# Host-packed per-feature vectors, one first stage with x loaded at its start, and projection weights in contiguous pieces

## The chip, the cores and the metric

The kernel runs on one core of one Trainium2 chip. A core has TensorE (PE), VectorE (DVE), ScalarE (ACT), GpSimd (POOL) and SyncE (SP), each with its own instruction stream, and 16 DMA engines. DMAs are issued here from SP's queue and from ScalarE's. The metric is the device time of one execution in microseconds (us), the median of the runs; less is better.

## The reference

A two-layer hybrid backbone serves 512 latent tokens and 128 context tokens of width 1024. Shortened to what matters here:

```python
def trunk_layer(x, mod, norms, mix_params, ffn, ctx):
    shift1, scale1, gate1, shift2, scale2, gate2 = jnp.split(mod, N_MOD, axis=-1)
    g_pre1, g_post1, g_pre2, g_post2 = norms
    h = rms_norm(x, g_pre1) * (1 + scale1) + shift1
    y, ctx_out = token_mixers(h, *mix_params, ctx=ctx)
    x = x + gate1 * rms_norm(y, g_post1)
    h = rms_norm(x, g_pre2) * (1 + scale2) + shift2
    return x + gate2 * rms_norm(ffn(h), g_post2), ctx_out

def token_mixers(h, w_in, conv_w, conv_b, ...):
    proj = h @ w_in                                    # (tokens, 1968)
    z, xbc, dt_raw, cq, ckv, k_rope = jnp.split(proj, ...)
    xbc = silu(centred_depthwise_conv(xbc, conv_w, conv_b))   # 5 taps
    ...                                                # chunked SSD scan
    q = rms_norm(cq, q_norm) @ w_uq
    ...                                                # latent attention
    return concatenate([rms_norm(y_ssd, ssd_norm), rms_norm(o, mla_norm)]) @ w_out
```

`mod` is SiLU(c) @ w_mod + b_mod, of 6 x 1024 values per layer, for `c` (latent tokens) and for `c_ctx` (context tokens). The feed-forward part is a dense SwiGLU in layer 0 and a top-2-of-8 expert SwiGLU in layer 1.

## The kernel before

All activations are float32. Tokens are tiled into five blocks of 128 (`TB` = 5; four latent, one context), features into eight of 128 (`KD` = 8). `build` (L2119) calls stages one after the other. Each stage is one block in which every engine has its own list of steps; semaphores (`Signal`) order steps of different engines, and a block ends when all of its engines have ended, so the stages are separated by barriers. Within a stage each engine takes its own list in order: a step that waits holds back all that is behind it in that list, DMA issues included.

The stages in order are: set-up, first modulation, and then for each layer pre-norm, input projection, SSD scan, attention, output projection, a second pre-norm, feed-forward and residual.

Set-up (`stage_setup`, L137) loads `c` and `c_ctx` feature-major into `silu_c` (values 4 bytes long, one per partition and column) on SP, builds identity and triangular masks on GpSimd, and takes SiLU on ScalarE.

First modulation (`stage_first_modulation`, L280) computes four units of 512 columns of `mod`: shift and scale of layer 0. The class `Modulation` holds this work in steps. `load` (on SP) brings each unit in four quarters of 128 x 1024 values (512 KB) into a ring of eight; a quarter past the eighth waits until TensorE has used the slots it replaces. `on_tensor` multiplies in two steps per unit (L230) and in a third transposes the unit's row (L218). `on_vector` copies the row out of PSUM (L240, `modrow`), and after the transposes sums it (L245) and adds the bias (L247), which needs `b_mod`. A unit's first product waits for the preceding unit's L247. `vectors` forms `scale_in` (L258). ScalarE issues ten loads of `b_mod` and gains in two layers, feature-major (L300, L302), then x_sample and x_prompt (L304, L305), then squares the five blocks of x (L428, through `squares_of`), and takes the root (L443). VectorE pads the SiLU values into `silu_wide`, makes float32r copies of two masks, waits for all ten small loads, runs the modulation steps and then `deviations` (L435 to L437), which turns sums of squares into `rstd`.

Pre-norm (`stage_pre_norm`) scales a diagonal by `rstd` (L397), multiplies each block of x by it (L382), evicts on VectorE (L411) and ScalarE (L364), and splits the result in a high and a low float32r part. SP loads the first two pieces of `w_in` (L473, class `InWeights`); in the input projection (`stage_in_proj`) it first issues five convolution tap rows and the bias (L511, L512), then pieces three to seven. A piece has 256 or 344 columns in eight row blocks; it is split on ScalarE (L478) and GpSimd (L482) and multiplied (L567, L570).

Attention (`stage_attention`) loads on SP `q_norm` (L1007), `kv_norm`, the rotary tables `cos` and `sin`, the cached latents and the weights, in this order; VectorE waits for the first four before it scales the latents (L1192). In layer 1 SP also writes zeros to the expert slots in DRAM. The output projection (`stage_out_proj`) loads `ssd_norm` and `mla_norm` (L1328, L1329), then four quarters of `w_out` (L1333), split in high and low parts on ScalarE and GpSimd (L1342); TensorE's products are L1404.

## Time and profile before

| | us |
|---|---|
| median of 3 runs | 2360.98 |
| lowest and highest | 2360.64, 2364.31 |
| the profiled execution, its time | 2356.16 |
| its span | 2354.4 |

| engine | busy us | share of the span |
|---|---|---|
| TensorE products | 2056.0 | 87% |
| VectorE | 1289.7 | 55% |
| ScalarE | 933.4 | 40% |
| GpSimd | 297.5 | 13% |

The page's list of DMA issues gives the time from issue to landing: 2.7 us for `c`, 8.0 us (median) for a quarter of `w_mod` in the first modulation, 8.2 us for x_sample and 8.9 us for x_prompt.

How to read the profile: times in rows are microseconds from the start of the span, unless marked ns. L240 is line 240 of the kernel before. A row of the timeline gives start, duration, engine, line, operation, written tile and read tiles, shapes, count, and in brackets the engine's idle time just before with what ended it. SPq and ACTq are the DMA queues of SyncE and ScalarE; the duration of a row with several issues runs from the first to the last. A row of stretches gives for each engine the busy time and the number of instructions, then the granted clock of TensorE as a share of 2.4 GHz, the busy share of the DMA engines (it can pass 1 in rounding), and the bytes moved. A busy time is no proof of a bound: what counts is which wait ends last in a stage.

### The profile page before, as it was taken

How to read it: one execution, taken by the hardware profiler on the slowest of the kernel's cores; microseconds unless marked ns; L12 is line 12 of the kernel's file. 1: busy time of each engine (PE TensorE's matmuls, PEld its weight loads, DVE VectorE, ACT ScalarE, POOL GpSimd, SP SyncE). 2: the span in 40 equal slices, each digit the busy share in tenths (PEclk: the TensorE clock that was granted, in tenths of full speed). 3: DMA queues.
4: the chain of work that ended last, by engine and by line, in shares of the span. 5: the costliest groups of instructions: out<-in, count | busy, mean ns of one | idle time of the engine just before them, and what ended most of it. 6: DMA issues, size and time to landing. Idle time of an engine off the chain costs nothing. (4 is left out here: it accounts for less than half of the span.)

```text
span 2354.4 us, 34297 instructions
## 1 busy us (share of the span) xinstructions
PE 2056.0 (87%) x12315; PEld 1777.1 (75%) x12315; DVE 1289.7 (55%) x1960; ACT 933.4 (40%) x1496; POOL 297.5 (13%) x128
## 2 busy tenths in 40 slices
PE   2898689985999999996998789797599999999992
PEld 1896447875999999996996448696487788778782
DVE  1735656654232022305817657643587888788884
ACT  1414203333221112104315103522577888788872
POOL 0220000031433233320320000300000000000001
PEclk9899899987999999997999899896799999999996
DMA  7315502110322122301306700201996835718444
GB/s 199 93 42 179 178 0 90 58 52 19 97 74 83 52 82 72 92 25 36 85 24 222 270 8 1 72 1 70 356 410 252 330 134 195 282 65 312 160 170 187
DMA packets 214206, 301.88 MB, mean 128 GB/s; under 512 B 52433, under 2 KB 143313, under 8 KB 214097
## 3 DMA queue, kind: packets, MB, share of 16 engines
q1 hardware_dynamic: 187744, 279.28, 33.8%
q10 hardware_dynamic: 23472, 10.57, 1.7%
q0 software_dynamic: 2880, 10.49, 1.1%
q8 instruction: 79, 1.29, 0.2%
q14 instruction: 31, 0.25, 0.0%
HBM read 358.20 MB, written 28.61 MB: 164 GB/s over the span
## 5 line engine op out<-in xcount | busy, mean ns | idle before, releaser
L1855 DVE TENSOR_TENSOR ex_wl<-ex_raw,ex_wh 128x1024 fp32r<-128x1024 f32 x364 | 425.3, 1219 | 57.7 <-ACT ex_wh L1734 53.7
L1734 ACT ACTIVATE ex_wh<-ex_raw 128x1024 fp32r<-128x1024 f32 x364 | 370.6, 1057 | 40.7 <-PE psum L1792 33.2
L1792 PE MATMUL psum<-ex_wh,ex_he_hi 128*128 128x512 f32 (+1 forms) x624 | 242.5, 389 | 5.1 <-DVE ex_wl L1855 5.1
L1792 PE MATMUL psum<-ex_wl,ex_he_hi 128*128 128x512 f32 (+1 forms) x624 | 233.3, 374 | 0.0
L1792 PE MATMUL psum<-ex_wh,ex_he_lo 128*128 128x512 f32 (+1 forms) x624 | 232.8, 373 | 0.0
L2001 POOL TENSOR_TENSOR ex_wl<-ex_raw,ex_wh 128x1024 fp32r<-128x1024 f32 (+1 forms) x60 | 160.6, 2679 | 338.4 <-ACT ex_wh L1987 338.4
L1044 ACT ACTIVATE at_prob<-psum,at_mx 128x640 f32<-128x640 f32 (+1 forms) x80 | 56.7, 708 | 307.2 <-DVE at_mx L1253 307.2
L2021 PE MATMUL psum<-h_hi,ex_wh 128*128 128x320 f32 x704 | 161.6, 311 | 16.7 <-POOL ex_wl L2001 15.3
L1987 ACT ACTIVATE ex_wh<-ex_raw 128x1024 fp32r<-128x1024 f32 (+1 forms) x60 | 68.4, 1141 | 259.9 <-PE psum L2021 243.0
L2021 PE MATMUL psum<-h_lo,ex_wh 128*128 128x320 f32 x704 | 161.3, 310 | 0.0
L2021 PE MATMUL psum<-h_hi,ex_wl 128*128 128x320 f32 x704 | 160.9, 310 | 0.0
L2049 DVE TENSOR_TENSOR ex_hf<-psum,ex_sg 128x640 f32<-128x640 f32 x22 | 18.1, 824 | 234.3 <-PE psum L2021 234.3
L1792 PEld LDWEIGHTS psum<-ex_wh,ex_he_hi 128*128 128x128 f32 x624 | 118.0, 189 | 27.7 <-issue 8.1
L1792 PEld LDWEIGHTS psum<-ex_wh,ex_he_lo 128*128 128x128 f32 x624 | 118.3, 190 | 21.9 <-issue 2.9
L1792 PEld LDWEIGHTS psum<-ex_wl,ex_he_hi 128*128 128x128 f32 x624 | 117.9, 189 | 21.0
L2021 PEld LDWEIGHTS psum<-h_hi,ex_wh 128*128 128x128 f32 x704 | 118.2, 189 | 17.2 <-issue 15.5
L2021 PEld LDWEIGHTS psum<-h_lo,ex_wh 128*128 128x128 f32 x704 | 118.5, 189 | 0.0
L2021 PEld LDWEIGHTS psum<-h_hi,ex_wl 128*128 128x128 f32 x704 | 118.5, 189 | 0.0
L1129 PE MATMUL psum<-mx_qkv_room,at_qT 96*128 96x320 f32 (+1 forms) x320 | 92.9, 416 | 13.8 <-DVE mx_qkv_room L1241 13.8
L1404 PE MATMUL psum<-op_w_hi,op_y_hi 128*128 128x256 f32 x320 | 93.2, 291 | 11.6 <-DVE op_y_lo L1431 11.4
L567 PE MATMUL psum<-win_hi,hm_hi 128*128 128x344 f32 (+1 forms) x320 | 96.4, 301 | 0.0
L567 PE MATMUL psum<-win_hi,hm_lo 128*128 128x344 f32 (+1 forms) x320 | 96.3, 301 | 0.0
(368 smaller groups left out, 4492.2 us busy)
## 6 DMA issues: line engine op xcount, KB each, us to landing
ex_raw<-moe_gate_up SPq DMA_DIRECT2D x286, 512.0 KB
ex_raw<-moe_w_down SPq DMA_DIRECT2D x78, 512.0 KB
x<-moe_w_down SPq DMA_DIRECT2D x65, 512.0 KB
wmod_ssd<-w_mod SPq DMA_DIRECT2D x56, 512.0 KB, 5.9
wmod_at<-w_mod SPq DMA_DIRECT2D x24, 512.0 KB, 4.9
ex_raw<-ffn_w_gate SPq DMA_DIRECT2D x22, 512.0 KB, 3.7
ex_raw<-ffn_w_up SPq DMA_DIRECT2D x22, 512.0 KB, 3.8
ex_raw<-ffn_w_down SPq DMA_DIRECT2D x16, 704.0 KB, 4.6
```

The costliest lines, as they stand in the source:

```text
L567: last = pe.matmul(p.psum[:, g % 8, 0:width], mh[:, k, j * P:(j + 1) * P], mw[:, k, :], start=first, stop=final)
L1044: act.activation(prob[:, n % 2, 0:hi - lo].rearrange("p (a k) -> p a k", a=2), p.psum[:, 2 * (n % 2):2 * (n % 2) + 2, 0:w], ACT.Exp, bias= ...
L1129: last = pe.matmul(p.psum[:, 2 * (n % 2) + part, 0:w], qT[0:QD, h, b * P:(b + 1) * P], kT[0:QD, h, lo + part * w:lo + (part + 1) * w], sta ...
L1404: last = pe.matmul(out, y[:, b % 2, k, :], w[:, i, k, :], start=(k == 0 and n == 0), stop=(k == KD - 1 and n == 2))
L1734: act.activation(wh[:, i % RING], raw_of(i), ACT.Copy).then_inc(*hi_done.up(1))
L1792: last = pe.matmul(p.psum[:, 2 + g % 2, 0:width], h[:, k], w[:, i % RING, cols], start=(k == 0 and m == 0), stop=(k == KD - 1 and m == 2))
L1855: dve.tensor_tensor(wl[:, i % RING], raw_of(i), wh[:, i % RING].bitcast(F32), ALU.subtract).then_inc(*lo_done.up(1))
L1987: act.activation(wh[:, SLOT[i], 0:size(i)], raw[:, i % 2, 0:size(i)], ACT.Copy).then_inc(hi_done, 1)
L2001: ins = pool.tensor_tensor(wl[:, SLOT[i], 0:size(i)], raw[:, i % 2, 0:size(i)], wh[:, SLOT[i], 0:size(i)].bitcast(F32), ALU.subtract)
L2021: last = pe.matmul(p.psum[:, 2 * PAIR[i] + half, 0:HT], w[:, SLOT[i], cols], m[:, k, half * HT:(half + 1) * HT], start=(k == 0 and n == 0) ...
L2049: ins = dve.tensor_tensor(hf[:].rearrange("p (a c) -> p a c", a=2), halves, sg[:].rearrange("p (a c) -> p a c", a=2), ALU.mult)
```

## The change

The host packs the following into one array `vectors` of 128 x 270 values: `c` and `c_ctx`, and for both layers `b_mod`, four gains, the convolution's taps and bias, `q_norm` and the norms of the two head groups. The kernel loads it once, on SP, and the tiles that held them become views of it. The set-up stage and the first modulation become one stage. In it SP issues the vectors and then `w_mod`; ScalarE issues x first, then takes SiLU, then squares x; VectorE does `deviations` before the modulation's steps instead of after them. The small loads of `stage_in_proj`, `stage_attention` (`q_norm`) and `stage_out_proj` go, with their waits. `w_mod`, `w_in` and `w_out` are laid out by the host so that each piece that is loaded is contiguous: 4 KB to 11 KB for each partition instead of runs of 1 to 2 KB. At the end of SP's list in attention a wait is added for the zeros that it wrote. No arithmetic of the reference moves to the host.

The diff, shortened; the GpSimd steps of set-up stand unchanged in the new stage.

```diff
+        self.vectors = sb("vectors_sb", [P, VECTOR_COLS])
+        self.silu_c = self.vectors[:, 0:2 * KD].rearrange("p (k s) -> p k s", k=KD)
...
@@ Modulation.load
             sp.dma_start(self.w[:, i % self.ring].rearrange("p (k f) -> p k f", k=QK),
-                         self.p.io["w_mod"][l, q * QK * P:(q + 1) * QK * P, u * UNIT:(u + 1) * UNIT].rearrange(
-                             "(k p) f -> p k f", p=P)).then_inc(*self.landed[i % self.ring].up(16))
+                         self.p.io["w_mod"][l, u, q].rearrange("p (k f) -> p k f", k=QK)
+                         ).then_inc(*self.landed[i % self.ring].up(16))
@@ stage_first_modulation
             @block.sync
             def _(sp):
+                sp.dma_start(p.vectors[:], io["vectors"]).then_inc(*vectors_in.up(16))
                 mod.load(sp)
...
             @block.scalar
             def _(act):
-                with nc.allow_non_contiguous_dma(reason="bias and gains, feature-major"):
-                    for l in range(2):
-                        act.dma_start(p.b_mod[:, l], io["b_mod"][l].rearrange("(k p) -> p k", p=P)).then_inc(*small.up(16))
-                        for j, name in enumerate(("norm_pre_mix", "norm_post_mix", "norm_pre_ffn", "norm_post_ffn")):
-                            act.dma_start(p.gains[:, l, j], io[name][l].rearrange("(k p) -> p k", p=P)
-                                          ).then_inc(*small.up(16))
                 act.dma_start(p.x[:, 0:LB], ...)
                 act.dma_start(p.x[:, LB], ...)
+                act.wait_ge(*vectors_in.at(16))
+                act.activation(p.silu_c, p.silu_c, ACT.Silu).then_inc(*silu_done.up())
                 for b in range(TB):
                     squares_of(p, act, b, junk[:], x_in.at(32), squared)
                 root_of_means(p, act, mean, root)
...
             @block.tensor
             def _(pe):
                 pe.wait_ge(*wide_ready.at(1))
+                pe.wait_ge(*consts.at(1))
...
             @block.vector
             def _(dve):
                 link = chained(dve_c)
-                pad_conditioning(p, link, dve, wide_ready)
+                link(dve, dve.memset(p.silu_wide[:], 0.0))
+                dve.wait_ge(*consts.at(1))
                 dve.tensor_copy(p.far_r[:], p.far[:])
                 dve.tensor_copy(p.ident_r[:], p.ident[:])
-                dve.wait_ge(*small.at(160))
+                dve.wait_ge(*silu_done.at(1))
+                dve.tensor_copy(p.silu_wide[:, :, 0:2], p.silu_c).then_inc(*wide_ready.up())
+                deviations(p, dve, squared, mean, root)
                 for step in range(len(mod.steps)):
                     mod.on_vector(dve, step)
                 mod.vectors(dve, link, 0, 0, ("scale",))
-                deviations(p, dve, squared, mean, root)
@@ InWeights.load
-        sp.dma_start(self.by_block(self.raw, i), self.p.io["w_in"][self.l, :, lo:hi].rearrange(
-            "(k p) f -> p k f", p=P)).then_inc(*self.landed[i % 2].up(16))
+        sp.dma_start(self.by_block(self.raw, i), self.p.io["w_in"][
+            self.l, :, KD * self.OFFSETS[i]:KD * self.OFFSETS[i + 1]].rearrange("p (k f) -> p k f", k=KD)).then_inc(...)
@@ stage_in_proj
-                    for k in range(TAPS):
-                        sp.dma_start(cw[:, :, k], io["conv_w"][l, k].rearrange("(f p) -> p f", p=P)).then_inc(*small.up(16))
-                    sp.dma_start(cb[:], io["conv_b"][l].rearrange("(f p) -> p f", p=P)).then_inc(*small.up(16))
                 for i in pieces[2:]:
                     w.load(sp, i)
...
-                act.wait_ge(*small.at(16 * (TAPS + 1)))
-                dve.wait_ge(*small.at(16 * (TAPS + 1)))
@@ stage_attention
-                    sp.dma_start(gq[:], io["q_norm"][l].rearrange("(k p) -> p k", p=P)).then_inc(*gains_in.up(16))
...
+                    sp.wait_ge(slots["cleared"], 16 * (MAX_BLOCKS + 1))
                 sp.wait_ge(*new_out.at(32))
...
-                dve.wait_ge(*gains_in.at(64))
+                dve.wait_ge(*gains_in.at(48))
@@ stage_out_proj
-                    sp.dma_start(gain[:, 0:4], io["ssd_norm"][l].rearrange("(k p) -> p k", p=P)).then_inc(*small.up(16))
-                    sp.dma_start(gain[:, 4:8], io["mla_norm"][l].rearrange("(k p) -> p k", p=P)).then_inc(*small.up(16))
-                    sp.dma_start(raw[:, i % 2], io["w_out"][l, :, i * quarter:(i + 1) * quarter].rearrange(
-                        "(k p) f -> p k f", p=P)).then_inc(*landed[i % 2].up(16))
+                    sp.dma_start(raw[:, i % 2], io["w_out"][l, i].rearrange(
+                        "p (k f) -> p k f", k=KD)).then_inc(*landed[i % 2].up(16))
...
-                dve.wait_ge(*small.at(32))
@@ build
-        stage_setup(p)
         stage_first_modulation(p)
@@ on the host
+def projection_pieces(a):
+    rows = a["w_in"].reshape(2, KD, P, IN_COLS).transpose(0, 2, 1, 3)
+    a["w_in"] = np.concatenate([rows[..., lo:hi].reshape(2, P, KD * (hi - lo)) for lo, hi in InWeights.PIECES], axis=2)
+    quarters = a["w_out"].reshape(2, KD, P, 4, D // 4).transpose(0, 3, 2, 1, 4)
+    a["w_out"] = np.ascontiguousarray(quarters.reshape(2, 4, P, KD * D // 4))
+    units = a["w_mod"].reshape(2, QUARTERS, QK, P, UNITS, UNIT).transpose(0, 4, 1, 3, 2, 5)
+    a["w_mod"] = np.ascontiguousarray(units.reshape(2, UNITS, QUARTERS, P, QK * UNIT))
```

## Rows read from the trace of the kernel before

**Rows 1.** Stretches: busy by engine PE, PEld, DVE, ACT, POOL; clock; DMA; GB/s

```profile
0.00:55.50 55.50, 14.65 (x80) 3.79 (x80) 5.50 (x19) 8.75 (x14) 2.31 (x13) 0.99 0.80 200
...
76.40:188.20 111.80, 111.10 (x768) 110.92 (x768) 52.93 (x63) 23.59 (x29) 32.40 (x9) 0.98 0.21 57
```

**Rows 2.** Waits before 56 us: who <- for whom: us, times, longest

```profile
ACT fm_junk L428 <- DMA x<-x_prompt: 40.5, 1, 40.5
DVE modrow_first L240 <- DMA gains<-norm_post_ffn: 31.6, 1, 31.6
```

**Rows 3.** Timeline, DMA issues: start, us, queue, line, destination<-source

```profile
0.79 0.45 SPq L146 DMA_DIRECT2D silu_c<-c  x1
...
4.55 39.65 SPq L209 DMA_DIRECT2D wmod_first<-w_mod  x16
...
5.05 20.41 ACTq L302 DMA_DIRECT2D gains<-norm_pre_mix  x1
...
35.06 0.61 ACTq L304 DMA_DIRECT2D x<-x_sample  x1
35.69 0.53 ACTq L305 DMA_DIRECT2D x<-x_prompt  x1
```

**Rows 4.** Timeline, first modulation: start, us, engine, work, [idle before <-releaser]

```profile
37.11 0.69 DVE L240 COPY modrow_first<-psum 128x512 f32<-128x512 f32 x1 [31.62 <-DMA gains<-norm_post_ffn]
...
39.45 3.64 PE L230 MATMUL psum<-wmod_first,silu_wide_first 128*32 128x512 f32 x16 [0.48 <-DVE mod L247]
...
44.61 1.06 ACT L428 ACTIVATE fm_junk<-x 128x1024 f32<-128x1024 f32 x1 [40.49 <-DMA x<-x_prompt]
...
45.05 1.92 PE L230 MATMUL psum<-wmod_first,silu_wide_first 128*32 128x512 f32 x16 [0.48 <-DVE mod L247]
...
48.92 2.20 PE L230 MATMUL psum<-wmod_first,silu_wide_first 128*32 128x512 f32 x16 [0.48 <-DVE mod L247]
...
50.31 0.18 ACT L428 ACTIVATION_READ_ACCUMULATOR fm_junk<-x 128x1 f32 x1
...
53.04 0.17 DVE L258 SCALAR_TENSOR_TENSOR scale_in<-mod,gains 128x16 f32<-128x16 f32 x1
53.25 0.17 DVE L435 TENSOR_SCALAR stat<-stat 128x5 f32<-128x5 f32 x1
...
55.52 0.48 DVE L397 TENSOR_SCALAR pn_diagonal<-ident,rstd 128x128 f32<-128x128 f32 x2 [0.30 <-PEq L290]
```

**Rows 5.** Stretches of 5 us: last column GB/s

```profile
5.00:10.00 5.00, 0.00 (x0) 0.00 (x0) 0.49 (x3) 0.00 (x0) 0.00 (x0) 1.00 0.93 225
...
20.00:25.00 5.00, 0.00 (x0) 0.00 (x0) 0.00 (x0) 0.00 (x0) 0.00 (x0) 1.00 1.11 342
...
40.00:45.00 5.00, 3.75 (x20) 0.81 (x12) 1.05 (x3) 0.39 (x1) 0.00 (x0) 1.00 1.03 412
```

**Rows 6.** Stretch in which the granted clock (PEclk) falls

```profile
54.00:55.00 1.00, 0.00 (x0) 0.00 (x0) 0.00 (x0) 0.99 (x2) 0.00 (x0) 0.53 0.00 0
```

**Rows 7.** Timeline, around and in the first pre-norm

```profile
51.92 0.66 PE L218 MATMUL psum<-ident,modrow_first 128*128 128x128 f32 x4 [0.80 <-DVE modrow_first L240]
...
59.69 0.46 ACT L364 ACTIVATE pn_h<-psum,mod,scale_in 128x128 f32<-128x128 f32 x1 [4.69 <-PE psum L382]
...
66.54 2.05 PE L382 MATMUL psum<-pn_diagonal,x 128*128 128x128 f32 x16 [0.75 <-DVE pn_diagonal L397]
```

**Rows 8.** Timeline, input projection: issue of the third piece

```profile
79.97 20.93 SPq L473 DMA_DIRECT2D mx_qkv_room<-w_in  x3
```

**Rows 9.** Waits of TensorE from 76 to 190 us

```profile
PE psum L570 <- PEq L340: 7.8, 1, 7.8
```

**Rows 10.** Timeline, first layer's attention

```profile
266.81 0.38 SPq L1007 DMA_DIRECT2D at_gq<-q_norm  x1
...
271.64 0.48 DVE L1192 SCALAR_TENSOR_TENSOR mx_ckr<-mx_ckr,at_rstd,at_kvrow 128x256 f32<-128x256 f32 x1 [3.07 <-DMA at_sin<-rope_sin]
```

**Rows 11.** Waits of TensorE in the second layer's output projection

```profile
PE psum L1404 <- POOL op_w_lo L1342: 0.3, 1, 0.3
```

More of the change, by code:

```diff
@@ L50 @@
 FAR = -1e30
+VECTORS = (("b_mod", NMOD * KD), ("gains", 4 * KD), ("conv_taps", XF * TAPS), ("conv_bias", XF), ("q_norm", QR // P),
+           ("group_norms", KD))
+LAYER_COLS = sum(n for _, n in VECTORS)
+VECTOR_COLS = 2 * KD + 2 * LAYER_COLS
 class Signal:
@@ L96, in __init__ @@
         self.far_r, self.ident_r = sb("far_r", [P, 2, P], F32R), sb("ident_r", [P, P], F32R)
-        self.silu_c = sb("silu_c", [P, KD, 2])
+        self.vectors = sb("vectors_sb", [P, VECTOR_COLS])
+        self.silu_c = self.vectors[:, 0:2 * KD].rearrange("p (k s) -> p k s", k=KD)
         self.mod = sb("mod", [P, 2, NMOD * KD, 2])
-        self.b_mod = sb("b_mod_t", [P, 2, NMOD * KD])
-        self.gains = sb("gains", [P, 2, 4, KD])
+        by_layer = self.vectors[:, 2 * KD:].rearrange("p (l c) -> p l c", l=2)
+        views, at = {}, 0
+        for name, n in VECTORS:
+            views[name] = by_layer[:, :, at:at + n]
+            at += n
+        self.b_mod = views["b_mod"]
+        self.gains = views["gains"].rearrange("p l (j k) -> p l j k", j=4)
+        self.conv_taps = views["conv_taps"].rearrange("p l (f t) -> p l f t", f=XF)
+        self.conv_bias, self.q_norm, self.group_norms = views["conv_bias"], views["q_norm"], views["group_norms"]
         self.scale_in = sb("scale_in", [P, 2, 2, KD, 2])
@@ L282, in stage_first_modulation @@
     nc, io = p.nc, p.io
-    x_in, small, dve_c = p.sig("x_in"), p.sig("mod_small"), p.sig("dve_chain")
-    wide_ready = p.sig("silu_wide_ready")
+    x_in, vectors_in, dve_c = p.sig("x_in"), p.sig("vectors_in"), p.sig("dve_chain")
+    consts, pool_chain, silu_done, wide_ready = (p.sig(n) for n in (
+        "consts", "pool_chain", "silu_done", "silu_wide_ready"))
     squared, mean, root = p.sig("x_squared"), p.sig("x_mean"), p.sig("x_root")
@@ L452 @@
     WIDEST = max(hi - lo for lo, hi in PIECES)
+    OFFSETS = [0, *itertools.accumulate(hi - lo for lo, hi in PIECES)]
     def __init__(self, p, l, raw_room, ctx):
@@ L501, in stage_in_proj @@
     with ExitStack() as own:
[L502 removed]
+        cw, cb = p.conv_taps[:, l], p.conv_bias[:, l]
         pad = p.sb(f"conv_pad{l}", [P, 2, PADW], ctx=own)
@@ L508, in _ @@
             def _(sp):
-                with nc.allow_non_contiguous_dma(reason="small per-channel vectors"):
-                    for k in range(TAPS):
-                        sp.dma_start(cw[:, :, k], io["conv_w"][l, k].rearrange("(f p) -> p f", p=P)).then_inc(*small.up(16))
-                    sp.dma_start(cb[:], io["conv_b"][l].rearrange("(f p) -> p f", p=P)).then_inc(*small.up(16))
                 for i in pieces[2:]:
@@ L1005, in _ @@
             def _(sp):
-                with nc.allow_non_contiguous_dma(reason="one gain per partition"):
-                    sp.dma_start(gq[:], io["q_norm"][l].rearrange("(k p) -> p k", p=P)).then_inc(*gains_in.up(16))
                 sp.dma_start(kvrow[:], io["kv_norm"][l].partition_broadcast(P)).then_inc(*gains_in.up(16))
@@ L1299, in stage_out_proj @@
     nc, io = p.nc, p.io
-    landed, small = [p.sig(f"weights_landed{i}") for i in range(2)], p.sig("wo_small")
+    landed = [p.sig(f"weights_landed{i}") for i in range(2)]
     hi_done, lo_done, y_out = p.sig("weights_hi"), p.sig("weights_lo"), p.sig("yt_out")
@@ L1326, in _ @@
             def _(sp):
-                with nc.allow_non_contiguous_dma(reason="one gain per partition"):
-                    sp.dma_start(gain[:, 0:4], io["ssd_norm"][l].rearrange("(k p) -> p k", p=P)).then_inc(*small.up(16))
-                    sp.dma_start(gain[:, 4:8], io["mla_norm"][l].rearrange("(k p) -> p k", p=P)).then_inc(*small.up(16))
                 for i in range(4):
@@ L2219 @@
     arrays["rope_cos"], arrays["rope_sin"] = rope_tables()
+    arrays["vectors"] = small_vectors(arrays)
+    projection_pieces(arrays)
     arrays["moe_gate_up"] = expert_pieces(arrays.pop("moe_w_gate")[0], arrays.pop("moe_w_up")[0])
```

72 lines of the change are left out of this document (36 added, 36 removed).

## The prediction

> **What bounds the kernel now.** I read four views, in this order. First the page's chain that ended last: nearly all of what it names is TensorE work of the expert stage, which the diff doesn't touch, so its shares don't answer the question. The stages stand one behind the other between barriers, so a stage that ends earlier moves all behind it by the same amount; each touched stage is therefore read alone, in the table of stretches. The first 55.5 us (set-up and first modulation) hold only 14.65 us of TensorE work, while the input projection is busy for 111.10 of 111.80 us [rows 1]. An earlier load can pay in the first and not in the second. Then the waits of the first stretch: ScalarE waits 40.5 us for `x_prompt`, VectorE 31.6 us for the last gain vector [rows 2]. The queue listing shows why. ScalarE's DMA queue starts with ten feature-major vectors (4-byte runs), and they block it: the issue of one gain takes 20.41 us, x_sample is issued at 35.06, x_prompt at 35.69 [rows 3]. Last the order of work in that stretch: two chains start late and end together. The modulation runs from the copy of unit 0's row at 37.11 to `scale_in`, 53.04 + 0.17 = 53.21. The norm runs from x landed (44.61) through five squares, to 50.31 + 0.18 = 50.49, and its next step stands on VectorE behind the modulation: 53.25 to 55.22, which is 0.30 before the next stage's first VectorE work at 55.52 [rows 4].
>
> **Part 1, vectors in one load, x first.** Removed: the ten vector loads ahead of x, and with them both waits of [rows 2]. Added: one load of 128 x 1,080 B ahead of w_mod on SP's queue. At the 2.7 us that c took it lands at 3.5, and even at twice that silu ends by 7 us, long before x. What is late next is x, since the change also puts `deviations` ahead of the modulation's VectorE steps: a new wait. Behind it on VectorE stand all twelve modulation steps, and TensorE waits for them from unit 0's transposes on. So the path is: x landed, norm, then the whole modulation.
> - x landed. Before, x took 44.61 - 35.06 = 9.55 us from its first issue [rows 3, 4]. 2.62 MB of x and an estimated 0.33 MB of w_mod went through in that time; at 0.41 MB/us, the mean of 40 to 45 us, once the 4-byte traffic is gone (342 GB/s with it beside [rows 5]), this is 7.2 us of transfer and 2.35 us fixed. After, both queues start at 0.79 [rows 3] and x meets eight w_mod quarters of 0.52 MB. Ends: x has the engines to itself, issued at 1.4 and landed 44.61 - 35.69 = 8.9 us later, at 10.3; or it is served behind all eight, 6.95 MB, 0.79 + 2.35 + 17.0 = 20.1. I take equal shares: 2 x 2.62 + 0.14 = 5.38 MB, 13.1 us, 0.79 + 2.35 + 13.1 = 16.2, less 0.2 for its head start: 16.0. The nearest row is x's own load, at whose end both queues had work too.
> - Norm: squares 50.49 - 44.61 = 5.9, mean to reciprocal 55.22 - 53.25 = 2.0 [rows 4]: VectorE free at 23.9.
> - Modulation: 53.21 - 37.11 = 16.1, less 0.3, the excess of unit 3's 2.20 over 1.92, which I read as its last quarters held up by x [rows 4]: 15.8, end 39.7. At 23.9 us at most twelve quarters and x, 9.05 MB, are asked for, 22 us of transfer; unit 2 needs the last of them some 8 us later. The modulation isn't bound by its loads.
> - Barrier 0.3: first VectorE work of the next stage at 40.0 instead of 55.52. Gain 15.5.
> Masks and silu now run inside this stage, under the load of x. Without that cover they would cost at most the 3.8 us between 0.79 and 4.55, the first issues of the two stages [rows 3].
>
> The Trainium skill (DMA: Bandwidth & Descriptors, "Where 436 GB/s comes from") puts loads from HBM at about 358 GB/s per core. By that x would land 1.9 us later (5.38/0.358 = 15.0 us against 13.1). The trace disagrees: 412 GB/s over five microseconds [rows 5]; the measurement decides. The same page ("Queues, rings and completion order") says that each DMA engine goes round its queues packet by packet, which would give the equal shares; no row isolates this for two queues of long runs.
>
> **Part 2, TensorE's clock at the next stage.** Before, TensorE's last transposes end at 51.92 + 0.66 = 52.58 and the granted clock falls early in 54 to 55 us (mean 0.53), to the 1.2 GHz level [rows 6]; the pre-norm starts cold and its first block is evicted at 59.69, 4.17 us after 55.52. Warm (2.4 GHz), a block's 16 records take 2.05 us [rows 7]; with 0.3 for the diagonal and 0.1 for the release that is 2.5. After, the norm's tail no longer stands between: the idle time is 0.63 (to `scale_in`'s end) + 0.3 + 0.3 = 1.2 us, under the 1.4 after which the clock fell, so I take it as warm: 1.7 us, and 0.3 of the second block's wait. Gain 2.0. Ends: 0 (it falls all the same) and 2.0. Inside the modulation unit 1 took 3.64 us and unit 2 1.92 [rows 4], which I read as cold and warm; a rise at another moment gains up to 1.7 or costs as much. I take none of that.
>
> **Part 3, input projections, both layers.** Six small loads go from ahead of the third piece, which is issued at 79.97 in a stage that starts at 76.4: 3.6 us of SP's queue [rows 8]. The cover is TensorE: its one wait from 76 to 190 us is the one for the stage's start [rows 9]. So nothing is gained; were the cover gone, it would be 3.6 us each. Contiguous pieces land earlier under the same cover, and so do the modulation weights of later stages. Gain 0; bounds -0.5 to +0.5 per layer.
>
> **Part 4, attention and output projection.** In attention VectorE's first scaling waits until 271.64 for the load of `sin`; ahead of it on SP's queue goes one issue of 0.38 us and its gap, 0.43 [rows 10], in two layers: 0.9. In the output projection of the second layer TensorE waits 0.3 us for a low part of w_out [rows 11]; w_out is now issued a microsecond earlier, its two gain loads gone: 0.3. The first product there waits for VectorE's `y_lo`, not for weights. The added wait for `cleared` ends SP's list in attention, with nothing of its stage behind it, and the stores it waits for are issued at the stage's beginning. Nothing.
>
> **Sum.** 15.5 + 2.0 + 0 + 0.9 + 0.3 = 18.7 us. The profiled execution has a span of 2354.4 and a time of 2356.16; after: 2335.7 and 2337.5. It ran 4.8 us under the median of the three runs, 2360.98; from that median: 2342.3.
>
> **Rivals.** (a) x nearly alone, landed at 10.3: 5.7 us more, 2336.6. For it: x is two issues, while w_mod's quarters go out one by one. Against: by 5 us both queues are full. (b) x behind w_mod, landed at 20.1: 4.1 us less, 2346.4; behind all twelve quarters at 25: 2351.3. For it: more is queued on SP. (c) As forecast, but the clock falls before the pre-norm: 2344.3; with (b) 2348.4. (d) Slower: the new wait itself. All of the modulation stands behind x; 7.9 + 15.8 + 0.3 us after x must still be before 55.52, so from x landed at 31.5 us on the first stage loses. That takes twelve quarters ahead of x and under 0.31 MB/us: at 225 GB/s, the mean of 5 to 10 us [rows 5], 9.05 MB land at 43.4, and the time is 2360.98 + 11.9 - 3.2 = 2369.7. Against: the 4-byte loads that stood beside that rate are gone. (e) The change doesn't do what its words say: contiguous w_mod, w_in and w_out bring nothing. That is already in the forecast; what carries it is ScalarE's queue [rows 3].
>
> **Chances.** Forecast 0.45, (c) 0.17, (a) 0.14, (b) 0.15, (d) 0.03, something that gives the gain back later 0.06. The range goes from (a) with an earlier rise of the clock, 2335, to (b) with (c) and some scatter of the median, 2350. A measurement of this kernel can tell about 0.2% (4.7 us) from no change: faster 0.93, same 0.04, slower 0.03.
>
> **What would show it.** The squares of x start near 16 us (10 to 20); the first `modrow` copy 7.9 us later; `pn_diagonal` near 40; a granted clock of 1.00 through the first pre-norm block, evicted 2.5 us after `pn_diagonal`; an input projection as long as before; attention's first scaling 0.43 us earlier in its stage. The prediction is wrong if the modulation waits for w_mod in units 1 to 3, if x is starved, or if a later stage grows.

## The result, and the profile after

The changed kernel takes 2345.32 us (median; 2338.96 to 2349.9), the kernel before 2360.81 in the runs beside it. The ratio is 0.9933, 95% interval 0.991 to 0.9955: 15.5 us faster. The forecast was 2342.3, with a range of 2335 to 2350. So sign, range and rough size hold. One step does not: two later stages give back 10 us by the traces, where the forecast had a gain of 0.3.

The profiled execution of the changed kernel was the slowest of its four (span 2348.1, time 2349.9), that of the kernel before (2356.16) quicker than all four of its other times. A second trace of the kernel before was taken for that reason (e10); its span is 2357.2. The table cuts both at the starts of the stages, read from the first DMA issue of each. In all listings below, rows between those shown are left out.

| stage | before, 2nd trace, us | after, us | difference | forecast |
|---|---|---|---|---|
| set-up and first modulation | 57.17 | 39.61 | -17.56 | -15.5 |
| pre-norm, input projection, layer 0 | 133.24 | 130.30 | -2.94 | -2.0 |
| SSD scan, layer 0 | 78.73 | 78.59 | -0.14 | 0 |
| attention, layer 0 | 197.75 | 196.31 | -1.44 | -0.43 |
| output projection, layer 0 | 115.19 | 119.63 | **+4.44** | 0 |
| up to layer 1's pre-norm | 522.78 | 522.90 | +0.12 | 0 |
| pre-norm to SSD scan, layer 1 | 212.14 | 212.44 | +0.30 | 0 |
| attention, layer 1 | 185.89 | 186.87 | +0.98 | -0.43 |
| output projection, layer 1 | 105.02 | 110.84 | **+5.82** | -0.3 |
| router, experts, end | 749.29 | 750.61 | +1.32 | 0 |
| whole span | 2357.2 | 2348.1 | -9.1 | -18.7 |

The first four rows bring 22.1 us, the two output projections cost 10.3. What is left, 2.7 us, is spread over four rows; 1.0 of it is attention in layer 1.

The stretches of the changed kernel that answer to [rows 1]; columns are length, then busy time and count of TensorE, its weight loads, VectorE, ScalarE, GpSimd, then granted clock, DMA share, GB/s:

```profile
0.00:39.60 39.60, 15.95 (x80) 4.35 (x80) 5.49 (x19) 8.73 (x14) 2.31 (x13) 1.00 0.71 282
58.20:169.90 111.70, 111.04 (x768) 110.84 (x768) 51.26 (x63) 23.70 (x29) 32.06 (x9) 0.98 0.17 57
```

The same engine work stands in 39.6 us instead of 55.5, and the input projection is as long and as full as it was. The waits before 40 us, answering to [rows 2] (who, for whom: us in total, times, longest):

```profile
ACT fm_junk L418 <- DMA x<-x_prompt: 10.3, 1, 10.3
...
DVE stat L425 <- ACT fm_junk L418: 16.0, 1, 16.0
```

ScalarE's wait of 40.5 us is 10.3 now. VectorE's wait for gains is gone, and the squares of x take its place. The timeline of that stage, answering to [rows 3, 4, 6, 7]:

```profile
13.98 1.06 ACT L418 ACTIVATE fm_junk<-x 128x1024 f32<-128x1024 f32 x1 [10.33 <-DMA x<-x_prompt]
...
19.88 0.17 DVE L425 TENSOR_SCALAR stat<-stat 128x5 f32<-128x5 f32 x1 [16.02 <-ACT fm_junk L418]
21.77 0.65 DVE L213 COPY modrow_first<-psum 128x512 f32<-128x512 f32 x1
24.08 3.64 PE L203 MATMUL psum<-wmod_first,silu_wide_first 128*32 128x512 f32 x16 [0.48 <-DVE mod L220]
30.14 2.97 PE L203 MATMUL psum<-wmod_first,silu_wide_first 128*32 128x512 f32 x16 [0.48 <-DVE mod L220]
35.07 1.93 PE L203 MATMUL psum<-wmod_first,silu_wide_first 128*32 128x512 f32 x16 [0.48 <-DVE mod L220]
38.93 0.17 DVE L231 SCALAR_TENSOR_TENSOR scale_in<-mod,vectors_sb 128x16 f32<-128x16 f32 x1
39.65 0.48 DVE L387 TENSOR_SCALAR pn_diagonal<-ident,rstd 128x128 f32<-128x128 f32 x2 [0.55 <-PEq L264]
42.08 1.50 ACT L354 ACTIVATE pn_h<-psum,mod,scale_in 128x128 f32<-128x128 f32 x4 [20.45 <-PE psum L372]
```

x lands at 13.98, the modulation starts 7.8 us later, its units 1 to 3 wait for VectorE and never for `w_mod`, and the first pre-norm block is evicted 2.43 us after `pn_diagonal`, at full clock:

```profile
35.00:40.00 5.00, 2.59 (x21) 0.85 (x21) 1.59 (x7) 0.00 (x0) 0.00 (x0) 1.00 0.00 0
40.00:42.00 2.00, 2.00 (x18) 2.00 (x19) 0.13 (x1) 0.00 (x0) 0.00 (x0) 1.00 0.69 168
```

Attention's first scaling, answering to [rows 10], starts at 252.44 in a stage that starts at 248.50: 3.94 us into it instead of 4.83; in layer 1, 3.89 instead of 4.29.

Now the stage that grows: layer 0's output projection in the changed kernel, by its timeline.

```profile
444.81 22.46 SPq L1313 DMA_DIRECT2D mx_qkv_room<-w_out  x4
449.60 1.89 POOL L1319 CAST op_w_hi<-mx_qkv_room 128x2048 fp32r<-128x2048 f32 x1 [200.53 <-DMA mx_qkv_room<-w_out]
451.57 4.50 POOL L1322 TENSOR_TENSOR op_w_lo<-mx_qkv_room,op_w_hi 128x2048 fp32r<-128x2048 f32 x1
452.75 3.34 DVE L1394 TENSOR_SCALAR op_stat<-op_stat 128x10 f32<-128x10 f32 x1
...
462.40 9.42 POOL L1322 TENSOR_TENSOR op_w_lo<-mx_qkv_room,op_w_hi 128x2048 fp32r<-128x2048 f32 x2 [6.33 <-ACT op_w_hi L1343]
...
467.50 5.40 DVE L1409 TENSOR_TENSOR op_y_lo<-op_yf,op_y_hi 128x1024 fp32r<-128x1024 f32 x1
...
472.95 0.58 PE L1384 MATMUL psum<-op_w_hi,op_y_hi 128*128 128x256 f32 x1 [10.15 <-DVE op_y_lo L1409]
```

Look at the ends, not the starts. A step on ten columns (`op_stat`, the mean of the squares) takes 3.34 us; it ends at 456.09, and GpSimd's first subtraction (`w_lo` of the first quarter of `w_out`) at 456.07. `y_lo` takes 5.40 us and ends at 472.90; the second and third subtraction run back to back (9.42 us) until 471.82, so it gets through 1.08 us after them. In the first trace of before the same two steps of this layer take 0.17 and 1.23 us. Between them stands the cast of `y_hi`, which is held as well (3.86 us; 0.69 where GpSimd is idle), but it was so in before too (3.77), so it is no part of the difference. The first product of the stage comes 28.1 us after its start (28.7 in layer 1), where it came after 21.8 and 21.1. TensorE's waits there:

```profile
PE psum L1384 <- DVE op_y_lo L1409: 10.2, 1, 10.2
...
PE psum L1369 <- ACT mx_xst L1338: 8.9, 1, 8.9
```

These two were 5.7 and 5.8 us in before: 4.5 and 3.1 us more, the two stalls one behind the other. All products of the stage then take 60.3 and 61.3 us instead of 62.6, so the stage as a whole loses 4.4 and 5.8 us and not 6.3 and 7.6. The granted clock helps in layer 0 alone, by some 0.8 us (it stays at the 1.2 GHz level for the first 3.1 us of the products instead of 4.7; in layer 1 for 5.2 instead of 3.6). What both layers share is a pace: at a granted clock of 1.00 a block of 96 products takes 11.46 us here and 11.76 in before. What that goes with is said under "What e3 adds".

### The profile page after: what moved, and what is told of

It reads as the page before. It is cut to its first block and busy times, and to the rows that moved or that the text cites. A ratio compares the mean times of both kernels' runs of the same rounds, so it can differ in the third digit from the quotient of the medians.

```text
span 2348.1 us, 34267 instructions
## 1 busy us (share of the span) xinstructions
PE 2051.2 (87%) x12315; PEld 1772.3 (75%) x12315; DVE 1305.1 (56%) x1960; ACT 934.9 (40%) x1496; POOL 294.3 (13%) x128
## 3 DMA queue, kind: packets, MB, share of 16 engines
q1 hardware_dynamic: 141488, 279.36, 32.7%
## 5 line engine op out<-in xcount | busy, mean ns | idle before, releaser
L2036 DVE TENSOR_TENSOR acc<-acc,psum 128x640 f32<-128x640 f32 x16 | 13.2, 822 | 149.6 <-PE psum L1999 149.6
```

## The experiments

Two theories stood at first. **P** (a conflict of VectorE and GpSimd): `w_out` lands earlier in its stage (its first quarter 4.79 us after the stage's start, before about 7.2), so GpSimd's subtractions come to lie on VectorE's two short steps, which then end only with them. **C:** the 10 us are scatter of the profiled executions, or a clock that fell. Later a third question came up: which part of the change carries the first stage's gain.

### e1: the changed kernel once more

> The changed kernel once more, beside which the others of this call are read. In its trace TensorE's first product of the output projection comes 28.2 us (layer 0) and 28.8 us (layer 1) after w_out's first issue, against 20.8 and 20.5 before; VectorE's op_stat took 3.34 and 4.26 us instead of 0.17 and 0.34, its op_y_lo 5.40 instead of 1.23. Theory P (a conflict of VectorE and GpSimd): the same again in every execution, since w_out's landing sets it, so the time is again about 15 us under before. Theory C (TensorE's clock and scatter between executions): the stage lengths differ from the first trace by several us in either direction.

Measured: 2345.98 us, ratio 0.9946 (0.9929 to 0.9962). `op_stat` 3.33 and 4.18 us, `y_lo` 5.40 twice, first product 28.15 and 28.77 us after the issue. The stalls are the same to 0.1 us in both layers: not scatter. C falls for them.

### e2: the output projection as it was before

```diff
+                    sp.dma_start(gain[:, 0:4], io["ssd_norm"][l]...)   # and mla_norm
-                    sp.dma_start(raw[:, i % 2], io["w_out"][l, i].rearrange(
-                        "p (k f) -> p k f", k=KD))...
+                    sp.dma_start(raw[:, i % 2], io["w_out"][l, :, i * quarter:(i + 1) * quarter].rearrange(
+                        "(k p) f -> p k f", p=P))...
...
+                dve.wait_ge(*small.at(32))
```

> The changed kernel with its output projection as before: w_out in rows of 1 KB and two gain loads issued ahead of it. Theory P: the first quarter lands 1.4 to 2 us later in its stage, GpSimd's first subtraction starts behind op_stat, the third one behind op_y_lo, both VectorE steps are short again (0.2 and 1.2 us), the first product comes 6 to 7 us earlier in each layer, and the time falls by 11 to 13 us against the changed kernel, about 27 us under before. Theory C: no change against the changed kernel beyond scatter (2 to 3 us).

Measured: 2337.08 us, ratio 0.9906 (0.9889 to 0.9923), 8.9 us less than e1, where 11 to 13 were expected. In the traces the two output projections are 11.4 us shorter than in e1; the first stage is 1.8 us shorter as well, which the edit doesn't touch (see Part 1). In its timeline the cast of the first quarter comes 7.25 us after the stage's start (443.76) instead of 4.79, and the stalls are gone:

```profile
451.01 1.89 POOL L1322 CAST op_w_hi<-mx_qkv_room 128x2048 fp32r<-128x2048 f32 x1 [203.00 <-DMA mx_qkv_room<-w_out]
451.75 1.18 DVE L1397 TENSOR_SCALAR op_stat<-op_stat 128x10 f32<-128x10 f32 x1
...
464.34 1.22 DVE L1414 TENSOR_TENSOR op_y_lo<-op_yf,op_y_hi 128x1024 fp32r<-128x1024 f32 x1
```

First product 20.87 and 20.42 us after the first issue for `w_out`. The give-back is made in this stage by this part of the change: the layout of `w_out` and the two gain loads with their tile `op_gain` of 128 x 8 values. e4 takes the first of these alone. (`op_stat` is 1.18 here because the cast lies on it until 452.90; that is short enough not to matter.)

### e3: the order held by two waits

The same kernel as the changed one, with contiguous `w_out` and its early landing kept; GpSimd may start the first subtraction only after `op_stat`, and the third only after `y_lo`.

```diff
                 for i in range(4):
                     pool.wait_ge(*hi_done.at(i + 1))
+                    if i == 0:
+                        pool.wait_ge(*mean.at(1))
+                    if i == 2:
+                        pool.wait_ge(*y_out.at(1))
```

> The changed kernel, in which GpSimd waits with its first subtraction for op_stat and with its third for the first op_y_lo; w_out lies as in the changed kernel. Theory P: as with the output projection of before, first product 6 to 7 us earlier per layer, 11 to 13 us off the changed kernel's time. A theory L (the contiguous layout itself makes w_out's later quarters slow) expects the third and fourth quarter to land late here too and no gain. Theory C: none either.

Measured: 2329.60 us (2328.03 to 2330.99), ratio 0.9876 (0.9859 to 0.9893), 16.4 us less than e1.

```profile
451.43 0.16 DVE L1398 TENSOR_SCALAR op_stat<-op_stat 128x10 f32<-128x10 f32 x1
451.74 4.51 POOL L1326 TENSOR_TENSOR op_w_lo<-mx_qkv_room,op_w_hi 128x2048 fp32r<-128x2048 f32 x1 [1.40 <-DVE op_stat L1398]
...
462.99 1.23 DVE L1413 TENSOR_TENSOR op_y_lo<-op_yf,op_y_hi 128x1024 fp32r<-128x1024 f32 x1
464.27 0.58 PE L1388 MATMUL psum<-op_w_hi,op_y_hi 128*128 128x256 f32 x1 [6.08 <-DVE op_y_lo L1413]
464.36 4.58 POOL L1326 TENSOR_TENSOR op_w_lo<-mx_qkv_room,op_w_hi 128x2048 fp32r<-128x2048 f32 x1 [1.96 <-DVE op_y_lo L1413]
```

Two waits that let the long instruction go second give back more than the whole of the loss: the stages take 111.1 and 101.2 us, against 119.6 and 110.8 in the changed kernel and 115.2 and 105.0 in before. Against before a stage is thus some 4 us shorter once nothing stands in the way of the early `w_out`: the first product comes up to a microsecond earlier, the products are 2 us shorter. Not all of that is the early `w_out` (see "What e3 adds"). P had expected 11 to 13 us, only the loss undone.

### e4: contiguous `w_out` alone, in the kernel before

```diff
-                    sp.dma_start(raw[:, i % 2], io["w_out"][l, :, i * quarter:(i + 1) * quarter].rearrange(
-                        "(k p) f -> p k f", p=P))...
+                    sp.dma_start(raw[:, i % 2], io["w_out"][l, i].rearrange(
+                        "p (k f) -> p k f", k=KD))...
```

> The kernel before with one part of the change: w_out in contiguous quarters, its two gain loads kept. Nothing is gained elsewhere. Theory P: the first quarter lands about 0.6 us earlier, so GpSimd's first subtraction starts at 8.6 instead of 9.2 us of its stage, at or before op_stat at 8.9 (it then takes 4 us); the third quarter is there 0.6 us earlier, so that the gap between the second and third subtraction, 1.0 us, shrinks to 0.4 and op_y_lo may miss it: 0 to 8 us per layer slower, in all 4 to 15 us slower than before. Theory C: same time as before.

Measured: 2367.86 us (8 runs), ratio 1.0043 (1.0029 to 1.0058): slower than before by 8.6 us, by nothing but a layout. The first quarter lands 0.6 us earlier in layer 0, and 0.4 to 1.1 us earlier in layer 1, by the trace of before that it is set against. The two layers separate the stalls. Layer 0, then layer 1:

```profile
473.35 4.49 POOL L1342 TENSOR_TENSOR op_w_lo<-mx_qkv_room,op_w_hi 128x2048 fp32r<-128x2048 f32 x1
473.69 4.18 DVE L1414 TENSOR_SCALAR op_stat<-op_stat 128x10 f32<-128x10 f32 x1
...
489.28 5.40 DVE L1431 TENSOR_TENSOR op_y_lo<-op_yf,op_y_hi 128x1024 fp32r<-128x1024 f32 x1
...
1515.63 4.55 POOL L1342 TENSOR_TENSOR op_w_lo<-mx_qkv_room,op_w_hi 128x2048 fp32r<-128x2048 f32 x1
1515.64 0.17 DVE L1414 TENSOR_SCALAR op_stat<-op_stat 128x10 f32<-128x10 f32 x1
...
1526.92 4.61 POOL L1342 TENSOR_TENSOR op_w_lo<-mx_qkv_room,op_w_hi 128x2048 fp32r<-128x2048 f32 x1 [0.30 <-ACT op_w_hi L1363]
1527.21 5.41 DVE L1431 TENSOR_TENSOR op_y_lo<-op_yf,op_y_hi 128x1024 fp32r<-128x1024 f32 x1
```

In layer 0 both stall and the first product comes after 28.99 us. In layer 1 `op_stat` starts within 0.01 us of the subtraction and gets through in 0.17; only `y_lo` stalls, and the first product comes after 24.14. Against 20.8 and 20.1 in before that is 8.2 us for two stalls and 4.0 for one. The same two pairs in the kernel before, layer 0:

```profile
473.41 0.17 DVE L1414 TENSOR_SCALAR op_stat<-op_stat 128x10 f32<-128x10 f32 x1
473.64 4.51 POOL L1342 TENSOR_TENSOR op_w_lo<-mx_qkv_room,op_w_hi 128x2048 fp32r<-128x2048 f32 x1
...
484.98 1.23 DVE L1431 TENSOR_TENSOR op_y_lo<-op_yf,op_y_hi 128x1024 fp32r<-128x1024 f32 x1
485.36 5.28 POOL L1342 TENSOR_TENSOR op_w_lo<-mx_qkv_room,op_w_hi 128x2048 fp32r<-128x2048 f32 x1 [0.96 <-ACT op_w_hi L1363]
```

`op_stat` started 0.23 us ahead of the subtraction (0.39 in layer 1), `y_lo` 0.38 us ahead of the third one: by so little the kernel before missed the two stalls.

### e5: x first, alone, in the kernel before

```diff
+                act.dma_start(p.x[:, 0:LB], io["x_sample"]...).then_inc(*x_in.up(16))
+                act.dma_start(p.x[:, LB], io["x_prompt"]...).then_inc(*x_in.up(16))
                 (the ten vector loads, and after them no x)
```

> The kernel before with one part of the change: ScalarE issues its two loads of x ahead of the ten feature-major vector loads; nothing else moves. Theory Q (the queue of 4-byte loads is the bound, through both x and the gains): x lands near 11 to 16 us, but VectorE's first modrow copy still waits for the last gain, issued 1.1 us later than before, and lands at 37 to 39; the stage ends as before, 0 to 1.5 us slower. Theory X (x's late start alone is what the change repairs): up to 15 us faster.

Measured: 2364.0 us (10 runs), ratio 1.0022 (1.0011 to 1.0034): slower by 3.5 us of medians, where 0 to 1.5 were expected.

```profile
6.20 25.82 ACTq L304 DMA_DIRECT2D gains<-norm_pre_mix  x1
...
41.45 1.06 ACT L428 ACTIVATE fm_junk<-x 128x1024 f32<-128x1024 f32 x1 [37.22 <-issue]
...
43.69 0.69 DVE L240 COPY modrow_first<-psum 128x512 f32<-128x512 f32 x1 [38.09 <-DMA gains<-norm_post_ffn]
```

x is issued at 4.66 and has landed by 17.98, but ScalarE is held by its own issues of the 4-byte loads until 41.4 (the wait ahead of the squares is put down to issue, not to x's DMA), and the modulation waits for the last gain until 43.69, 6.6 us later than before (37 to 39 expected). So moving x gains nothing while the ten loads stand; what the first stage gained needs them gone. Packing the vectors alone, without the merged stages, wasn't run.

### e6: the norm inside the modulation

e3, with the `deviations` of the norm moved behind the steps of unit 0, where VectorE waits anyway.

```diff
-                deviations(p, dve, squared, mean, root)
                 for step in range(len(mod.steps)):
                     mod.on_vector(dve, step)
+                    if step == UNIT_STEPS - 1:
+                        deviations(p, dve, squared, mean, root)
```

> The changed kernel with GpSimd's subtractions held as in e3 and VectorE's deviations placed behind the steps of modulation unit 0 instead of ahead of them. In the changed kernel unit 0's products are done at 17.3 us and its row is copied only at 21.8, behind the norm. Theory W (this new wait costs 4.5 us): the first modrow copy starts near 17.4, the norm's steps run while TensorE works on unit 1, the pre-norm starts 4 to 4.5 us earlier and the time is about 4.5 us under e3, 34 under before. A rival expects less: units 1 to 3 then come before their w_mod quarters have landed (at the measured rate all 16 need until about 30 us), so that 0 to 2 us are won.

Measured: 2325.93 us, ratio 0.9852 (0.9835 to 0.9868), 3.7 us less than e3, where 4 to 4.5 were expected.

```profile
17.41 0.69 DVE L213 COPY modrow_first<-psum 128x512 f32<-128x512 f32 x1 [13.62 <-PE psum L203]
...
34.62 0.17 DVE L231 SCALAR_TENSOR_TENSOR scale_in<-mod,vectors_sb 128x16 f32<-128x16 f32 x1
```

The copy no longer waits for x but for unit 0's products and comes 4.3 us earlier than in e3; the wait for x that the change adds costs that much. The stage ends at 35.3 instead of 38.0: 1.6 us of it are lost again, since the modulation takes 17.4 us here and 15.8 in e3 (see Part 1).

### e7: high parts a block earlier

e6, with ScalarE converting each quarter's high part one block sooner.

> e6, and in the output projection ScalarE makes each high part of w_out one block earlier. In all traces so far GpSimd's second subtraction (14.4 to 18.9 us of the stage) holds VectorE's cast of y_hi (3.8 us instead of 0.7). Theory P: the subtraction now starts at 13.1 and ends at 17.6, the cast ends 1.3 to 1.9 us earlier, the first product too, and the time is 2.5 to 4 us under e6. Rival: the high parts become the bound (the third waits for w_out's landing ahead of block 2's scaling): no gain.

Measured: 2325.15 us (2324.38 to 2326.16), ratio 0.9848 (0.9832 to 0.9864), 0.8 us less than e6, inside the scatter, where 2.5 to 4 were expected. The second subtraction did move away from the cast of `y_hi` (2.63 us instead of 3.85), and the first product came at 19.55 and 19.70 us. But the turned blocks come later, since ScalarE's conversion now stands between them: TensorE's wait for `mx_xst` grows by 1.1 us while that for `y_lo` shrinks by 2.9.

```profile
PE psum L1375 <- ACT mx_xst L1343: 6.9, 2, 5.9
PE psum L1390 <- DVE op_y_lo L1415: 3.2, 1, 3.2
```

In e6 the two stood at 5.8 and 6.1. What the earlier first product gains (1.2 and 0.7 us) is mostly lost in the products, which take 61.2 us instead of 60.5: 5.0 us of them are at the 1.2 GHz level in both layers, against 3.6 and 3.1 in e6. This is the fastest kernel of the study by median, 1.5% under before, though e6 can't be told from it.

### e8: `w_mod` and `w_in` in rows again

e3, with the two weights in the layout of before; vectors, x and `w_out` as in the changed kernel.

> e3 with w_mod and w_in in rows as before (runs of 2 KB and 1 KB); x first, packed vectors and contiguous w_out stay. Theory N (contiguity of these two brings nothing, they are covered): x lands within 2 us of the 14 us of the changed kernel, the input projections are as long as before, the time is within 2 us of e3. Theory L (contiguous pieces are part of the gain in the first stage): 3 us or more slower than e3.

Measured: 2329.04 us, ratio 0.9863 (0.9846 to 0.9879); e3 had 2329.60. The contiguous `w_mod` and `w_in` bring nothing that can be measured. The trace shows two small effects that cancel:

```profile
12.68 1.06 ACT L418 ACTIVATE fm_junk<-x 128x1024 f32<-128x1024 f32 x1 [9.04 <-DMA x<-x_prompt]
...
34.89 1.07 PE L203 MATMUL psum<-wmod_first,silu_wide_first 128*32 128x512 f32 x8 [1.58 <-DMA wmod_first<-w_mod]
```

x lands 1.2 us earlier than in e3 beside 2 KB runs of `w_mod`, and unit 3 waits 1.58 us for its last quarters. TensorE's only wait in layer 0's input projection is again that for the stage's start, 7.8 us.

### e9: the two waits in the kernel before

> The kernel before, with the two waits of the third experiment alone: GpSimd starts a layer's first low part of w_out only after the deviations' mean, the third only after y_lo. In the kernel before, op_stat (0.17 and 0.34 us) and y_lo (1.23 us) were not held up, so the theory that the given-back time is VectorE standing behind GpSimd expects no change: ratio 0.998 to 1.001, first product 20 to 21 us after the first issue for w_out, in both layers. The rival, that the waits are worth something by themselves (so that the third experiment's 16 us would be partly theirs and not a give-back undone), expects 2 to 7 us less than before, seen in the two output projections.

Measured: 2359.38 us (11 runs), ratio 1.0001 (0.9992 to 1.001). The waits alone bring nothing; e3's gain is the change's own. The first product came 20.8 us after the first issue for `w_out` in both layers.

### e10 and e11: a second trace of before, a third of the changed kernel

> The kernel before, once more, for a second trace of it. Its first profiled execution (2356.2 us) stood 4.8 us under the median, and the traces of before and after differ by 6.3 us of span where their medians differ by 15.5. Theory: that is scatter between executions, not a stage; a second trace of before has a span of 2357 to 2361, its output projections are as in the first (first product 20 to 21 us after the first issue for w_out), and what differs from the first trace is spread over stages that the change doesn't touch. Rival: the first trace is typical of before (2353 to 2356 again), and the traces misstate the change.

> The changed kernel, a third trace. Its two traces so far stand 2.6 to 4.6 us over the median of its times. Theory: scatter again; span 2336 to 2349, the stall of op_stat (3.3 and 4.2 us) and of y_lo (5.4 us) as before in both layers, since they hang on the order of two engines and not on the execution. Rival: the fast executions of this kernel are those in which the stalls don't happen; then a trace under 2342 us shows op_stat at 0.2 us or y_lo at 1.2.

Measured: e10 2358.84 us, span 2357.2; e11 2347.92 us (2338.34 to 2351.16), span 2349.0, ratio 0.9945 (0.9927 to 0.9962). The first trace of before was a quick one, and the place is in the first stage, so "spread over stages that the change doesn't touch" was wrong: it takes 57.17 us in e10 (57.46 in e9), 55.47 in the first trace. The reason stands in e10's timeline, unit 3's two halves:

```profile
49.19 1.06 PE L230 MATMUL psum<-wmod_first,silu_wide_first 128*32 128x512 f32 x8 [0.61 <-DMA wmod_first<-w_mod]
51.74 1.07 PE L230 MATMUL psum<-wmod_first,silu_wide_first 128*32 128x512 f32 x8 [1.49 <-DMA wmod_first<-w_mod]
```

In the first trace this unit was one stretch of 2.20 us [rows 4]. e11's stages agree with the first trace after within 0.2 us up to the router, stalls included (3.26 and 4.27; 5.40 twice). It stays open why 3 of 15 executions of the changed kernel lie at 2338 to 2341 us, 4 us under the rest: no trace fell on one, so whether the stalls are missing there isn't known. Measured three times, the changed kernel's gain was 15.5, 13.2 and 11.2 us by medians.

## Why the prediction was right, and where it was wrong

**What bounds the kernel: right.** The first stage could pay and did; the input projection was full before and after.

**Part 1: right, from terms that miss both ways.** Expected: x at 16.0, VectorE free at 23.9, modulation 15.8, `pn_diagonal` at 40.0. Measured: 13.98, 21.77, 17.3, 39.65. Two terms were off:
- Equal shares of the two queues were too little for x. By 13.98 us, 336 GB/s, the mean from 0 on, had brought 4.70 MB; less x (2.62) and the vectors (0.14) that leaves 1.94 MB of `w_mod`, not 2.62. Both have runs of 4 KB. Beside the 2 KB runs of e8, 310 GB/s by 12.68 us make 3.93 MB, of which 1.17 were `w_mod`.
- Unit 2 ran 2.97 us, not 1.92: the slower pace of unit 1 lasted into it. The forecast read this pace as the 1.2 GHz level, and had named a rise at another moment as a scatter of up to 1.7 us either way. The stretches of the changed kernel show 1.00 from 24 to 33 us all the same. But the first clock record of that trace begins only at 32.30 us, and the view counts time without a record as 1.00. At that moment, inside unit 2, a single product falls from 1.06 to 0.59 us. In e8 the records begin at 16.9 us, and the stretch of its unit 1 has pace and clock in one row:

```profile
22.77:26.41 3.64, 3.64 (x16) 0.60 (x16) 0.00 (x0) 0.00 (x0) 0.00 (x0) 0.50 0.88 295
```

  Its unit 2 has sixteen products in 1.92 us at 1.00. So the pace is the clock, as the forecast read it. In e2 and e3 the first record begins at 27.9 and 27.6 us, ahead of unit 2; from first copy to `scale_in`'s end e3's modulation took 37.52 - 21.71 = 15.8. In the three traces of the changed kernel it begins at 32.3 to 32.7. The first stage is the same code in all five, so the 1.6 to 1.8 us by which it is shorter in e2 and e3 are no effect of their edits. In e6 the rise lies inside unit 2 again.

The price of the base was off as well: 55.5 was a quick first stage, 57.2 and 57.5 two later ones (e10, e9), so the gain was 17.6 and not 15.5. Of this the forecast had half the clue: it read unit 3's 2.20 as held up by `w_mod`, but took the size of that from the one trace.

The estimate by the Trainium skill's 358 GB/s (DMA: Bandwidth & Descriptors, "Where 436 GB/s comes from") falls here too: 410 GB/s from 5 to 10 us and 420 from 10 to 15 in the trace after. The Trainium skill (DMA: Bandwidth & Descriptors, "Queues, rings and completion order") lets each DMA engine go round its queues packet by packet. The two shares measured here agree with that in direction: halving `w_mod`'s runs cut its bytes per byte of x from 0.74 to 0.45.

**Part 2: right.** 2.43 us from `pn_diagonal` to the eviction (2.5 expected), clock 1.00. The stretch from there to the SSD scan shrank by 2.4 us against the first trace, 2.9 against the second; 2.0 was expected. Rival (c) didn't happen.

**Part 3: right.** 111.7 us against 111.8, and TensorE's one wait there is still 7.8 us; e8 shows that the layout is worth nothing in these two weights. That half of rival (e) holds. Its other half fails: contiguity of `w_out` did something, and it was a loss.

**Part 4, attention: right together, wrong in each layer.** The first scaling came 0.89 and 0.40 us earlier in its stage (0.43 expected), and the stages changed by -1.4 and +1.0 us: together -0.5 where -0.9 was expected. Neither is scatter: layer 0's attention takes 197.6 to 197.8 us in the five traces of kernels that load `q_norm` there and 196.2 to 196.3 in the other eight; layer 1's takes 185.8 to 185.9 in the five, and 186.8 to 187.6 in seven of the eight (185.8 in e7). What moves them beyond the 0.43 us is open.

**Part 4, output projection: wrong.** The step that failed reads: "The first product there waits for VectorE's `y_lo`, not for weights", from which the forecast concluded that an earlier `w_out` gains 0.3 us and nothing else. The first half is true and was the warning. It asked only who waits for `w_out` on TensorE; it did not ask what GpSimd does with it the moment it lands, nor what stands on VectorE at that moment. The term was put at -0.3 us and measured +10.3 in the two layers. e2 (-8.9 us) places it in this stage, e4 (+8.6) in the layout alone, e3 (-16.4) in the order of two engines. Rows of the kernel before held the clue: `op_stat` started 0.23 us ahead of a 4.5 us subtraction, and `y_lo` started in a gap of 0.96 us between two others. The forecast's last line, "or if a later stage grows", and the 6% for a gain given back later are where the outcome lay; 6% was far too little.

**The sum.** Against the trace it was drawn from, the forecast wanted -18.7 and got -6.3. Against a typical trace of before (e10) it is -9.1: more than forecast in the first four rows (22.1 against 17.9) and +10.3 given back. By the medians, which the forecast was made for, it is -15.5 the first time and -13.2 and -11.2 on repetition. That 2342.3 lay only 3.0 us from 2345.3 is partly luck: a mis-sized loss, and gains that were larger than forecast. A right term for the output projections on the same sum would have given 18.7 - 10.6 = 8.1 us and 2352.9, above the range.

**What e3 adds.** P had expected the same of e2 and e3. That e3 is 7.5 us better than e2 shows what the loss had covered: the stages are 3.6 and 3.7 us shorter than in e2 (114.7 to 111.1, 104.8 to 101.2, both from the stage's start). About 1 us of each is the first product's. The rest goes with products that take 60.7 and 60.3 us instead of 63.1 and 62.9, and two things make that difference. One is the granted clock: 3.6 and 3.0 us of the products are at the 1.2 GHz level instead of 6.0 and 5.7, which is worth 1.2 and 1.3 us. The other is the pace at full clock. The third block of 96 products in layer 0 (length; busy time and count of TensorE and of its weight loads; clock, DMA share, GB/s), in e4 and in e3:

```profile
520.95:532.71 11.76, 11.76 (x96) 11.55 (x96) 1.00 0.00 1
...
490.19:501.64 11.45, 11.45 (x96) 11.24 (x96) 1.00 0.01 1
```

Over the four blocks behind the first this is 1.2 us per layer. All six traces of kernels that keep `op_gain` in this stage (before, e2, e4, e5, e9, e10) have 11.76 for this block in both layers, the seven others 11.45 or 11.46. It isn't the layout, since e4 has the contiguous `w_out`; it isn't the packing elsewhere, since e2 has that. It goes with the two gain loads and their tile. The loads had landed long before these blocks, so a different place of the stage's tiles in SBUF is a guess; no run tests it. The forecast had no such gain, and it hides a part of what the stalls cost.

## What to carry to other kernels

A load that lands earlier starts its consumer earlier, and the consumer may hold something that a short step on the critical path needs. Before moving a load, list what each engine starts when it lands and what the other engines have in flight then, above all GpSimd's long instructions beside VectorE's short ones. If the order matters, write it as a wait of the long instruction on the short one: here two such waits turned a gain of 13 us into one of 30. And take a second trace of the base before pricing a stage by one.

## What the runs showed of the hardware

Three of VectorE's instructions between SBUF tiles don't finish while a GpSimd instruction that started first is under way. `op_stat` (TENSOR_SCALAR on 128 x 10 values) takes 0.16 us alone and 3.26 to 4.27 us with a subtraction of 4.5 us in flight. `y_lo` (TENSOR_TENSOR) takes 1.23 us alone and 5.40 with one. The cast of `y_hi` takes 0.69 us alone and 3.77 with one. It holds the other way round too: in before, `y_lo` ran from 484.98 to 486.21, the third subtraction started at 485.36 and took 5.28 us instead of 4.5. In e4's layer 1 `op_stat` and the subtraction started within 0.01 us of each other, and `op_stat` took 0.17. A held instruction is shown as busy and long, not as waiting.

Not every VectorE instruction is held. The gain steps that read PSUM (`op_yf`) took 2.16 us whether half of them (e11's and the first trace after) or all of them (e7) lay under a subtraction. The reciprocal behind `op_stat` has both its tiles in SBUF and took 0.22 us wholly under the subtraction that runs from 473.64 to 478.15 in before:

```profile
475.20 0.22 DVE L1416 RECIPROCAL op_rstd<-op_rstd 128x10 f32<-128x10 f32 x1 [1.61 <-ACT op_rstd L1354]
```

The Trainium skill (SBUF — State Buffer, "SBUF: two separate sides") states the rule: a port pair shared by VectorE and GpSimd is locked for a whole instruction by whoever comes first, and the other blocks; of VectorE's instructions it names those in a 2-port mode and those with two SBUF inputs. These rows agree with it, `y_lo` being one with two SBUF inputs; which of the others run in a 2-port mode no row shows. The forecast had not weighed it.

ScalarE's own work is held by its DMA issues ahead of it, which took long here with 4-byte runs: in e5 its queue stood at one such issue for 25.82 us, and its squares of x, which had landed by 17.98 us, began only at 41.45, when all ten vectors were issued.
